# Delta rounds of a two-block model: projections and constant products in column halves, the state's update in quarters, two levels one slot earlier

## What is computed

```python
def chunk_gated_delta_rule(q, k, v, g, beta):
    ...
    lower = jnp.where(strict, jnp.einsum('bhnik,bhnjk->bhnij', k_beta, kc) * decay, 0.0)
    t_inv = lax.linalg.triangular_solve(eye + lower, ...)
    u = t_inv @ v_beta
    w = t_inv @ (k_beta * jnp.exp(gc)[..., None])
    ...
    def step(state, xs):
        w_i, u_i, intra_i, qd_i, ks_i, gl_i = xs
        v_new = u_i - w_i @ state
        o_i = qd_i @ state + intra_i @ v_new
        state = state * jnp.exp(gl_i)[..., None, None] + jnp.swapaxes(ks_i, -1, -2) @ v_new
        return state, o_i
```

## Time and profile before

| | |
|---|---|
| median of 3 runs | 3288.83 us |
| the three runs | 3286.05, 3288.83, 3294.34 us |
| the profiled execution: span | 3288.9 us |
| TensorE busy | 3208.4 us, 98% |
| VectorE, ScalarE, GpSimd busy | 1625.7, 786.2, 371.5 us |
| delta rounds | about 1775 to 2335 us from the start |

### The profile page before, as it was taken

How to read it: one execution, slowest core, us unless ns; L and a number is a source line. 1 busy time by engine, 2 the same in 40 slices (tenths; PEclk the granted TensorE clock), 3 DMA queues, 4 the chain that set the end, 5 groups by cost and what they waited for, 6 DMA issues and landing times.

```text
span 3288.9 us, 45947 instructions
## 1 busy us (share of the span) xinstructions
PE 3208.4 (98%) x19506; PEld 2041.0 (62%) x19506; DVE 1625.7 (49%) x3199; ACT 786.2 (24%) x1796; POOL 371.5 (11%) x291
## 2 busy tenths in 40 slices
PE   7999989999999999999999999999999999999999
PEld 3456567888884757888887455555445548444444
DVE  5576765879642227779833666664223216010111
ACT  2333332211012026211002333332223212111111
POOL 0011121232010000122101111113000001100000
PEclk9999999999999999999999999999999999999999
DMA  6332112456641320266632111110211115899996
GB/s 217 122 92 73 55 57 78 128 174 196 193 141 40 90 77 1 64 182 190 185 86 78 52 39 40 39 35 6 80 52 45 52 52 205 338 421 420 421 421 265
DMA packets 355773, 452.49 MB, mean 138 GB/s; under 512 B 25712, under 2 KB 282992, under 8 KB 331760
## 3 DMA queue, kind: packets, MB, share of 16 engines
q1 hardware_dynamic: 355568, 449.55, 40.1%
HBM read 445.27 MB, written 4.20 MB: 137 GB/s over the span
## 4 chain that ended last, share of the span: by engine, by line
PE 88%; DVE 5%; DMA 4%; ACT 2%; issue 1%; POOL 0%; POOLq 0%; SPq 0%; DVEq 0%; ACTq 0%
PE bank L79 86%; DMA A<-in_w_up 2%; PE bank L82 2%; DMA W<-in_w_up 1%; ACT A L87 1%; DVE A L70 1%; DVE SM L76 1%; DVE A L76 1%; DVE H L70 0%; DVE A L73 0%; ACT SM L87 0%; DMA A<-in_x 0%; ACT H L87 0%; DVE A L2589 0%; DVE A L2591 0%
## 5 line engine op out<-in xcount | busy, mean ns | idle before, releaser
L79 PE MATMUL bank<-A 64*64 64x64 f32 (+6 forms) x8800 | 875.0, 281 | 30.4 <-DVE A L76 14.1
L79 PEld LDWEIGHTS bank<-A 64*64 64x64 f32 (+3 forms) x8800 | 676.9, 153 | 302.3 <-issue 89.6
L79 PE MATMUL bank<-A,W 128*128 128x256 f32 (+1 forms) x2240 | 723.7, 476 | 1.2 <-ACT A L87 0.7
L79 PE MATMUL bank<-H,W 128*128 128x512 f32 (+2 forms) x1712 | 648.6, 522 | 11.9 <-ACT H L87 7.8
L79 PEld LDWEIGHTS bank<-A,W 128*128 128x128 f32 x2240 | 415.7, 190 | 240.5 <-issue 200.8
L79 PEld LDWEIGHTS bank<-H,W 128*128 128x128 f32 (+1 forms) x1712 | 307.3, 189 | 246.9 <-issue 209.2
L87 ACT ACTIVATE A<-bank 128x512 f32<-128x512 f32 (+4 forms) x469 | 193.8, 418 | 1058.7 <-PE bank L79 1016.3
L79 PE MATMUL bank<-A,H 128*64 128x512 f32 (+2 forms) x1224 | 309.8, 573 | 4.8 <-DMA A<-in_w_up 3.4
L70 DVE TENSOR_TENSOR A<-bank,A 128x256 f32<-128x256 f32 (+1 forms) x350 | 157.2, 461 | 176.5 <-PE bank L79 171.1
L70 POOL TENSOR_TENSOR A<-A 128x512 f32<-128x512 f32 (+1 forms) x103 | 147.4, 1438 | 726.8 <-PE bank L82 356.4
L87 ACT ACTIVATE A<-A 128x512 f32<-128x512 f32 (+1 forms) x238 | 136.7, 610 | 356.7 <-DVE A L70 340.1
(11 more groups left out here) (191 smaller groups left out, 2656.3 us busy)
## 6 DMA issues: line engine op xcount, KB each, us to landing
A<-in_w_gate SPq DMA_DIRECT2D x47, 1024.0 KB, 23.9
W<-in_mod_w SPq DMA_DIRECT2D x45, 1024.0 KB, 5.4
A<-in_w_up SPq DMA_DIRECT2D x42, 1024.0 KB, 20.4
A<-in_w_down SPq DMA_DIRECT2D x35, 1024.0 KB, 27.0
W<-in_mlp_up SPq DMA_DIRECT2D x64, 512.0 KB, 5.3
W<-in_mlp_down SPq DMA_DIRECT2D x128, 256.0 KB, 4.0
W<-in_w_mod SPq DMA_DIRECT2D x24, 1024.0 KB, 5.2
W<-in_w_up SPq DMA_DIRECT2D x22, 1024.0 KB, 19.7
```

Source lines behind the costliest of these rows:

```text
L79: return self.e.matmul(o, l, r, start=start, stop=stop, skip_group_check=True)
```

## The change

`pe_halves` issues a product as two, one for each half of the output's partitions, with 64 columns of the stationary operand each. It replaces the full product in the fetch, in `dg`, `dss`, `doss` and `ssx`, and in the gate's projection of the late rounds; `pe_proj` gets the same as an option, which only the latent query's projection (`pe_cq`) uses. The state's update becomes four products of 64*64. In `pe_dscores` four counts of idle slots change, so that `du` of level 4 and `du` of level 5 stand one slot earlier and what is behind each stays.

```diff
-        def pe_proj(pe, key, src3, nk, n, banks, emptied, normed=None, width=256, steps=False):
+        def pe_proj(pe, key, src3, nk, n, banks, emptied, normed=None, width=256, steps=False, cut=128):
...
-                        m = pe.mm(BK[b][0:cw, :], v[:, kk, c:c + cw], src3[:, kk, :], kk == 0, kk == nk - 1)
+                        for c0 in range(0, cw, cut):
+                            c1 = min(c0 + cut, cw)
+                            m = pe.mm(BK[b][c0:c1, :], v[:, kk, c + c0:c + c1], src3[:, kk, :], kk == 0, kk == nk - 1)
...
+        def pe_halves(pe, b, l_, r_, start, stop):
+
+            for h in half:
+                m = pe.mm(b[h, :], l_[:, h], r_, start, stop)
+            return m
...
-                    m = pe.mm(BK[b][:, :], v[:, kk, :], h3[:, kk, :], kk == 0, kk == 7)
+                    m = pe_halves(pe, BK[b], v[:, kk, :], h3[:, kk, :], kk == 0, kk == 7)
...
-            pe.mm(BK[1][:, :], C("blk"), DG_, True, True).then_inc(s_pe, npe("dg", hd))
+            pe_halves(pe, BK[1], C("blk"), DG_, True, True).then_inc(s_pe, npe("dg", hd))
...
-                pe.mm(BK[3 + i][:, :], C("ones"), RW[i], True, True).then_inc(s_pe, npe("dss", hd, i))
+                pe_halves(pe, BK[3 + i], C("ones"), RW[i], True, True).then_inc(s_pe, npe("dss", hd, i))
...
                 tokens(n)
-                yield from idle(4 if n < 3 else 2)
+                yield from idle(4 if n < 3 else 1)
             pe.wait_ge(s_gp, ngp["dm", hd])
             pe.wait_ge(s_dv, ndv["dt", hd, 3])
             each(3, m8, DT).then_inc(s_pe, npe("du", hd, 4))
-            yield from idle(2)
+            yield from idle(3)
             pe.wait_ge(s_dv, ndv["dtt", hd, 3])
             pe.wait_ge(s_dv, ndv["da", hd, 4])
             each(4, TT, DA).then_inc(s_pe, npe("dt", hd, 4))
             each(3, DA, TT).then_inc(s_pe, npe("dtt", hd, 4))
-            yield from idle(2)
+            yield
             pe.wait_ge(s_ac, nac["dt", hd, 4])
             each(4, m8, DT).then_inc(s_pe, npe("du", hd, 5))
-            yield from idle(2)
+            yield from idle(3)
...
                 if s < 7:
-                    for n, h in enumerate(half):
-                        m = pe.mm(BK[5 + n][:, 256:384], KTk[h, s, :], U2s[s % 2][h, :], True, True)
+                    for d in half:
+                        for n, h in enumerate(half):
+                            m = pe.mm(BK[5 + n][d, 256:384], KTk[h, s, d], U2s[s % 2][h, :], True, True)
                     m.then_inc(s_pe, npe("dds", hd, s))
...
-            pe.mm(BK[2][:, :], C("ones"), OQ, True, True).then_inc(s_pe, npe("doss", hd))
+            pe_halves(pe, BK[2], C("ones"), OQ, True, True).then_inc(s_pe, npe("doss", hd))
...
-                    m = pe.mm(BK[0][:, :], wv(k, 0, (0, P), (8, 256))[:, kk, j % 2 * 128:j % 2 * 128 + 128], h3[:, kk, :], kk == 0, kk == 7)
+                    m = pe_halves(pe, BK[0], wv(k, 0, (0, P), (8, 256))[:, kk, j % 2 * 128:j % 2 * 128 + 128], h3[:, kk, :], kk == 0, kk == 7)
...
-            return pe_proj(pe, "cq", h3, KT, 512, (3, 4, 5, 6), lambda j: (s_ac, nac["cq", j]), steps=True)
+            return pe_proj(pe, "cq", h3, KT, 512, (3, 4, 5, 6), lambda j: (s_ac, nac["cq", j]), steps=True, cut=64)
```

More of the change, by code:

```diff
@@ L2744, in pe_dpost @@
                 pe.wait_ge(s_ac, nac["gdr", 1])
-                pe.mm(BK[0][:, :], C("ones"), SQG, True, True).then_inc(s_pe, npe("ssx"))
+                pe_halves(pe, BK[0], C("ones"), SQG, True, True).then_inc(s_pe, npe("ssx"))
             yield from idle(13)
```

## The result

The changed kernel takes 3267.03 us (median of 4 runs, 3259.19 to 3269.41) beside 3290.83 for the kernel before (4 runs, 3286.05 to 3294.34). The ratio is 0.9925 with a 95% interval of 0.9913 to 0.9938, so 24.7 us less, between 20 and 29; 23.5 were forecast, to 3265.4. The profiled execution has a span of 3267.3 us, 21.6 less than the one before. Its own time is 3269.41: in every run on record some 2 us of the time lie outside the span, before and after alike, so they cancel in differences.

The account below looks back on a forecast made before the run. TensorE, busy 98% of the span, was taken as the bound; savings of 4.1 + 9.4 + 3.7 + 1.9 + 3.3 + 1.1 = 23.5 us off 3288.9 gave 3265.4 us, range 3256 to 3278.

Parts of the forecast that it names:

- TensorE saves 7.9 - 4.25 - 0.2 = 3.45 us of work: Steady delta round: shape changes fall from 7.9 to 4.25 us, the state's updates cost 0.2 more; 3.45 us saved.
- the prices: TensorE's order: each change of tile shape costs about 0.15 us to a 64-wide shape, 0.20 to a 128-wide one.
- Rival one: State's update: four corners run two after two, 0.44 us an update; saving about 16.5 us, total 3272; chance 0.20.
- Rival four: Halved products: halves do not run side by side, 4 x 0.43 instead of 0.86 us each, adding 330 us; chance 0.02.
- a steady round ends 2.35 us earlier: Each of four steady delta rounds goes from 59.1 to 56.7 us, giving 9.4 us in all.
- the three places named: TensorE waits in a steady round: before du2 behind VectorE's turns, before du2 a chunk earlier, and at the last chunk's drk.
- the product of the last chunk: drk in a steady round, expected to wait for VectorE in the middle; 0.2 us taken off the saving.
- the round after: The delta round ending at 2222.47, behind the four steady ones: 3.7 us expected to be saved.
- the next: The delta round ending at 2272.30: 3.1 us saved on paper, 1.9 taken because TensorE waits there.
- The last part: The last delta round, 3.3 us, and the rest of the last chain with the four blocks of cq, 1.1 us.
- a piece of each round that isn't TensorE: Round's end behind du2: ScalarE copies, VectorE turns two operands, then forms dx; TensorE's shorter work in these 6.4 us gains nothing.
- Rival two: Delta rounds: nothing is swallowed, all of TensorE's saving arrives, 31 us, total 3258; chance 0.07.

Follow-up runs that it names:

- the kernel of the three moves: The changed kernel with convolution taps, turns of the solved blocks and scalings of q and k later in VectorE's order, TensorE's order untouched; 3254.35 us, ratio 0.9887.
- the second experiment: The changed kernel with only the projection of the delta heads (dq) put back to full 128*128 products; 3282.53 us, ratio 0.9973.

## Why the prediction was right, and where not

**TensorE's work: right.** "TensorE saves 7.9 - 4.25 - 0.2 = 3.45 us of work" measured 58.69 - 55.27 = 3.42, and with each part undone the work moved by 0.61 (update; 0.6 by the prices), 2.96 (projection; 3.2) and 1.25 (constants; 1.25). A change to a 64-wide shape measured 0.13 to 0.15, to a 128-wide one 0.185 where 16 were undone. Rival one is refuted: the update's streams take 0.22. The traces agree with the rule of the Trainium skill ("TensorEngine Tiling (Array Packing)", Key Properties) that different tiles load and multiply in parallel. The roughly 62 ns on a matmul that the Trainium skill ("TensorE: Matmul & The Clock Gate", Wait — 56ns, not 53.3ns?) names for hardware decode off do not show: the records of level 4 begin 0.27 us after the first of the update's eight, where eight times 62 ns would be 0.50. Rival four is refuted by 0.215 a record.

**What reaches the end: a term mis-sized.** Here a part was too high. That "a steady round ends 2.35 us earlier" measured 2.09. The three waits are at the three places named, 0.86 ("about 0.9") and 0.49 ("about 0.5"), but the product of the last chunk waits 0.40, not the 0.2 that I took off. Four rounds gave 8.3 instead of 9.4. The rest was mostly short too: without the clock 3.1 instead of 4.1 before the first of them, 3.3 instead of 3.7 for the round after. For the next I had 1.9 and it gave 0.5: TensorE now idles 2.50 us until 2204.84, and from 2205.6 the clock is at 1.2 GHz for 3.4 us, which costs 1.7 (the 0.97 of the last row of the stretches); without that it is 2.2. The last part gave 4.2 of 4.4. In all 21 of the 23.5 came without the clock. What failed is the sentence that the chain behind du2 has "a piece of each round that isn't TensorE" as far as it treats that piece as given. The copies and turns stayed in the kernel of the three moves, but dx went ahead of the turns: the wait came from what was written ahead of dx, and a few idle counts removed it. Rival two, that nothing is swallowed, was false for this kernel; in the steady rounds it came true when VectorE's order was changed: on that order the work saved arrives whole, 58.62 - 55.27 = 3.35 a round.

**A term that the sum did not have: the clock.** The parts without it are 21 us, 2.5 short of the forecast. The profile of before has a stretch at 1.2 GHz, half of the full clock, 10.2 us long from 1784.8, in the first round of the delta rule. That of after has none: 5.1 us given here, 1.7 taken at 2205, so the delta stage became 24.5 us shorter. In the two profiled executions the one after had lost 2.1 us before the stage, with the low clock at other places there, and the stretch behind it gave back some 0.8 of what had arrived (22.4 ahead at 2336, 21.6 at the end); "Behind the rounds nothing takes it back" held but for that. That the forecast's 23.5 lies so near to 24.7 is in part luck, two errors that cancel. What was swallowed is read from the periods, not from the total.

## What to carry to other kernels

Count the changes of tile shape in TensorE's order, price each from two rows of the trace, and cut products so that neighbours share a shape: here a change cost 0.13 to 0.2 us, and the halves of an fp32 product of 128x512 streamed in the time of the whole one. Then look for what stands ahead of each awaited result in the other engines' written order. A saving on the engine that was the bound arrives whole only where the others wait for it, and moves that are worth next to nothing before the change were worth half of it after.

## What the runs showed of the hardware that was not expected

**The clock at the start of the delta rounds goes with full products.** Here is the stretch 1770 to 1830 in the kernel before, then in the changed one, in the one with the projection full again, and in the one with VectorE's order alone; the third number from the end is the clock.

```profile
1770.00:1830.00 60.00, 58.20 (x382) 32.88 (x381) 24.37 (x40) 20.91 (x39) 7.73 (x7) 0.91 0.26 70
```

```profile
1770.00:1830.00 60.00, 58.18 (x495) 26.81 (x493) 27.80 (x49) 22.21 (x40) 7.74 (x7) 1.00 0.27 71
```

```profile
1770.00:1830.00 60.00, 58.20 (x382) 31.82 (x381) 21.29 (x39) 20.91 (x39) 7.75 (x7) 0.89 0.26 70
```

```profile
1770.00:1830.00 60.00, 58.20 (x377) 32.79 (x377) 23.73 (x41) 21.43 (x39) 7.74 (x7) 0.89 0.26 71
```

In the three profiles with the projection in full products the clock is at 1.2 GHz there for 10.2, 13.7 and 13.7 us; of the ten with halves it stays at 2.4 in nine, and falls for 6.8 us in the one with the halves grouped. TensorE is as busy in either (58.20 and 58.18 of 60 us). The profiles are one execution of each kernel, but the mean granted clock is on record for nearly every timed run: 0.9893 over 53 runs of the three kernels with full projections and 0.9908 over 35 runs of the ten others. The difference of 0.0015 over some 3280 us is 5 us, an estimate that agrees with the 5.1 of the profiles. The projection's shape alone brings the stretch back (the second experiment changed nothing else); why a full product would do so is open, and no run here tests it. So some 5 us of this change's 24.7 are the clock and not the price of shape changes.

**Tiles do not need to alternate in the order.** Two first halves ahead of two second halves ran as fast as one after the other, but for 0.4 us in a round, in one execution. And **the four corners of the array run together**: 0.22 us for the update's eight records, where two products of 64*128 took 0.42 for their four with a change of 0.20, so 0.22 as well.
